# Decays between tokens in the SSD mixer: running sums spread over the partitions by a DMA, in place of triangle products

## The reference, cut to what matters

```python
A_cum = jnp.cumsum(dt * A, axis=2)                        # within a chunk
Acum_t = A_cum.transpose(0, 1, 3, 4, 2)
diff = Acum_t[..., :, None] - Acum_t[..., None, :]
Lmat = jnp.exp(jnp.where(causal, diff, -jnp.inf))         # decay from token s to token l
CB = jnp.einsum('bclgn,bcsgn->bcgls', Cc, Bc)
y_diag = jnp.einsum('bcgrls,bcsgrp->bclgrp', CB[:, :, :, None] * Lmat, xdt)
decay_states = jnp.exp(A_cum[:, :, -1:] - A_cum)
chunk_decay = jnp.exp(A_cum[:, :, -1])
y_off = jnp.einsum('bclgn,bcgrpn->bclgrp', Cc, S_prev) * jnp.exp(A_cum)[..., None]
```

## Time and profile before

| | |
|---|---|
| median of 3 runs | 2328.43 us (2327.97 to 2331.13) |
| the profiled execution | 2326.24 us, its span 2324.4 us |
| mean granted clock of TensorE in it | 0.966 |
| PE busy in the span | 2121.5 us (91%) |
| DVE | 1449.3 us (62%) |
| ACT | 974.8 us (42%) |
| POOL | 502.6 us (22%) |

### The profile page before, as it was taken

One profiled execution on the slowest core, in us unless ns is written; L12 is line 12 of the kernel. 1 busy time (PEld: TensorE's weight loads), 2 busy tenths in 40 slices (PEclk: granted clock), 3 DMA queues, 4 the chain that ended last, 5 costly groups with the idle time before them and its releaser, 6 DMA issues. The chain is left out here.

```text
span 2324.4 us, 43924 instructions
## 1 busy us (share of the span) xinstructions
PE 2121.5 (91%) x15061; PEld 1207.6 (52%) x15062; DVE 1449.3 (62%) x2501; ACT 974.8 (42%) x1470; POOL 502.6 (22%) x378
## 2 busy tenths in 40 slices
PE   7999999999979897999999999659999999999990
PEld 3455554555658873455555555325555555555450
DVE  7566565665668864344445454477566777777763
ACT  5432533333321333222222222147566677667653
POOL 0022121121220000001111011133333443444433
PEclk9999999999989999999999999879999999999995
DMA  8101001011050134112112110089889999999958
GB/s 254 51 28 64 1 28 64 1 28 48 10 227 28 56 127 173 55 37 73 46 64 73 37 46 37 37 305 353 256 277 315 325 342 347 344 336 332 343 167 305
DMA packets 160842, 350.96 MB, mean 151 GB/s; under 512 B 29866, under 2 KB 40490, under 8 KB 160464
## 3 DMA queue, kind: packets, MB, share of 16 engines
q1 hardware_dynamic: 140416, 311.37, 36.8%
q0 software_dynamic: 19152, 33.74, 6.4%
q10 hardware_dynamic: 1152, 4.19, 0.5%
HBM read 299.94 MB, written 58.26 MB: 154 GB/s over the span
## 5 line engine op out<-in xcount | busy, mean ns | idle before, releaser
L2690 PE MATMUL bankE<-wgu,xT 128*64 128x512 f16 x3840 | 429.9, 380 | 20.1 <-issue 11.7
L2690 PEld LDWEIGHTS bankE<-wgu,xT 128*64 128x64 f16 x3840 | 218.3, 110 | 223.1 <-issue 36.7
L2587 DVE SCALAR_TENSOR_TENSOR wgu<-w_rows,wgu 128x2048 f16<-128x2048 f32 x128 | 284.8, 2286 | 37.2 <-ACT wgu L2441 37.1
L111 PE MATMUL bankA<-main_room,hnT 128*128 128x512 f16 (+1 forms) x1536 | 303.2, 355 | 4.1 <-DVE main_room L646 4.1
L2389 POOL DMA_INDIRECT scratch_ybuf<-y,rows x80 | 173.2, 2165 | 376.6 <-DMA scratch_ybuf<-y,rows 276.5
L2441 ACT ACTIVATE wgu<-w_rows 128x2048 f16<-128x2048 f32 x128 | 234.3, 1899 | 34.4 <-issue 27.0
L111 PEld LDWEIGHTS bankA<-main_room,hnT 128*128 128x128 f16 x1536 | 149.9, 98 | 148.5 <-issue 10.3
L2690 PE MATMUL bankE<-wd,hT 128*64 128x512 f16 x1920 | 222.5, 381 | 0.4 <-ACT hT L2472 0.4
L2587 DVE SCALAR_TENSOR_TENSOR wd<-w_rows,wd 128x2048 f16<-128x2048 f32 x64 | 143.8, 2288 | 54.5 <-ACT wd L2441 51.7
L111 PE MATMUL bankA<-hnT,main_room 128*128 128x512 f16 x768 | 169.0, 381 | 8.9 <-issue 6.8
L111 PE MATMUL bankC<-w_out_s,catT 128*128 128x512 f16 x768 | 170.1, 382 | 2.5 <-DVE w_probs L2056 2.5
(11 more groups left out here) (390 smaller groups left out, 2992.1 us busy)
## 6 DMA issues: line engine op xcount, KB each, us to landing
w_rows<-in_w_gate SPq DMA_DIRECT2D x64, 1024.0 KB, 8.3
w_rows<-in_w_up SPq DMA_DIRECT2D x64, 1024.0 KB, 9.6
w_rows<-in_w_down SPq DMA_DIRECT2D x64, 1024.0 KB, 9.1
cat_t<-scratch_cat SPq DMA_DIRECT2D x16, 512.0 KB, 4.8
main_room<-in_x SPq DMA_DIRECT2D x16, 512.0 KB, 5.6
scratch_ybuf<-main_room SPq DMA_DIRECT2D x16, 512.0 KB, 2.6
out<-hf SPq DMA_DIRECT2D x16, 512.0 KB, 11.1
x_room<-in_x SPq DMA_DIRECT2D x3, 2048.0 KB, 10.9
```

Of the source, the lines that this page charges most:

```text
L111: ins = pe.matmul(o, a[x][k], b[y][k], start=start and k == 0 and j == 0, stop=stop and k == n - 1 and j == 2)
L2587: dve.scalar_tensor_tensor(place(p, slot, 1), room(p), W_SCALE, place(p, slot, 0), ALU.mult, ALU.subtract).then_inc(done, 1)
L2690: ins = pe.matmul(o(half), tokens(x, k), rows(z, k, half), start=k == 0 and j == 0, stop=k == n - 1 and j == 2, skip_group_check=True)
```

## The change

The running sums of a chunk are computed a second time as a row for each head: one product with `dtA` as the held operand and the triangle as the moving one gives 8 rows of 128 tokens. DVE copies the 8 rows out of PSUM, SP stores them (4 KB) into memory and loads them back onto all 128 partitions (512 KB, into `E`). ACT copies the running sums per token from PSUM into `cum`. DVE subtracts `cum` from the spread rows, head by head, cut at zero from above (8 operations), and ACT takes one exponential of 1024 columns in place. The triangle products, their two banks' turns in `BY`, and the laid out triangle go. The row of a group's first chunk is computed between the projections `project_vg` and `project_z` of that chunk; those of the other chunks in `retained` of the chunk before. SP's loop over groups is written out. A table of gains, 128 columns, becomes 2 columns that are read repeatedly.

```diff
-        SML = 12
+        SML = 10
-        gam = sb("gam", [P, 2 * RD])
+        gam = sb("gam", [P, 2])
+        cum = sb("cum", [P, SH])
+        row_own = sb("row_own", [SH, P])
...
-        BY = ["act", "act", "act", "act", "act", "dve", "dve", "dve", "dve", "dve", "dve", "dve"]
+        BY = ["act", "act", "act", None, None, "dve", "dve", "dve", "dve", "dve", "dve", "dve"]
...
+            def spread(q):
+                sp.wait_ge(row_taken, q + 1)
+                if q:
+                    sp.wait_ge(row_ld, q * 16)
+                sp.dma_start(row_scr.rearrange("(h l) -> h l", h=SH), row_own[:, :]).then_inc(row_st, 16)
+                sp.wait_ge(row_st, q * 16 + 16)
+                if q:
+                    sp.wait_ge(small, q * SML)
+                sp.dma_start(E[:, :, :].rearrange("p h l -> p (h l)"), row_scr.partition_broadcast(P)).then_inc(row_ld, 16)
...
             def decays(q):
                 act.wait_ge(small, q * SML + 3)
+                act.activation(cum[:, :], bank[SB0 + 2][:, 2 * SN:2 * SN + SH], ACT.Copy)
                 act.activation(dec[:, :, :], bank[SB0 + 2][:, 2 * SN:2 * SN + 3 * SH].rearrange("p (a b) -> p a b", a=3), ACT.Exp)
...
-            def segments(q):
-                for h in range(2):
-                    act.wait_ge(small, q * SML + 4 + h)
-                    act.activation(E2[:, h, :], bank[SB0 + h][:, :], ACT.Exp).then_inc(s_act, 1)
+            def exps(q):
+                act.wait_ge(diffs, q + 1)
+                act.activation(E[:, :, :], E[:, :, :], ACT.Exp).then_inc(e_done, 1)
...
-            def segments(q):
+            def take_row(q, room):
+                if q:
+                    dve.wait_ge(row_st, q * 16)
+                dve.tensor_copy(row_own[:, :], room).then_inc(row_taken, 1)
+
+            def first_row(q):
+                dve.wait_ge(row_done, q // GC + 1)
+                take_row(q, bank[SB0][0:SH, 0:P])
+
+            def differences(q):
+                dve.wait_ge(s_act, q * N_ACT + 3)
+                dve.wait_ge(row_ld, q * 16 + 16)
+                for h in range(SH):
+                    ins = dve.tensor_scalar(E[:, h, :], E[:, h, :], cum[:, h:h + 1], 0.0, ALU.subtract, ALU.min)
+                ins.then_inc(diffs, 1)
...
-                dve.tensor_tensor(segin[:, :, :], bc(le, 1, SH), bc(dtA[:, q % GC, :], 2, P), ALU.mult).then_inc(seg_ready, 1)
...
             def steps_decayed(q):
-                dve.wait_ge(s_act, q * N_ACT + 5)
+                dve.wait_ge(s_act, q * N_ACT + 3)
...
                 dve.wait_ge(s_dve, d0 + 1)
+                dve.wait_ge(e_done, q + 1)
...
+                if c < GC - 1:
+                    take_row(q + 1, bank[SB0][0:SH, RW:RW + P])
                 dve.tensor_copy(Y[:, c, 0:RW], bank[SB0][:, 0:RW]).then_inc(s_dve, 1)
...
-            def segments(q):
-                pe.wait_ge(seg_ready, q + 1)
-                for h in range(2):
-
-                    pe.matmul(room(q, 3 + h)[:, :], gt, sg2[:, h, :], start=True, stop=True).then_inc(small, 1)
+            def row(q, o):
+                pe.wait_ge(dt_ready, q + 1)
+                return pe.matmul(o, dtA[:, q % GC, :], le, start=True, stop=True)
+
+            def first_row(q):
+                row(q, room(q, 0)[0:SH, 0:P]).then_inc(row_done, 1)
...
+                if c < GC - 1:
+                    row(q + 1, o[0:SH, RW:RW + P])
...
+                    if part is project_vg:
+                        first_row(q0)
```

More of the change, by code:

```diff
@@ L375, in _ @@
                 sp.dma_start(late[kt % N_LR], w_in[kt * P:(kt + 1) * P, LATE]).then_inc(l_ld[kt % N_LR], 16)
-            with sp.Fori(0, NG - 1) as g:
+            def spread(q):
[7 more added lines that the diff above has]
+                sp.dma_start(E[:, :, :].rearrange("p h l -> p (h l)"), row_scr.partition_broadcast(P)).then_inc(row_ld, 16)
+            for g in range(NG - 1):
                 sp.wait_ge(big, g * BIG + KT)
-                sp.dma_start(xg[:, :, :], xv[bass.ds(g + 1, 1)].squeeze(0)).then_inc(x_ld, 16)
+                sp.dma_start(xg[:, :, :], xv[g + 1]).then_inc(x_ld, 16)
+                for c in range(GC):
+                    spread(g * GC + c)
                 sp.wait_ge(qk_free, g * GC + GC)
-                sp.dma_start(rope[:, :, :], rv[bass.ds(g + 1, 1)].squeeze(0)).then_inc(r_ld, 16)
+                sp.dma_start(rope[:, :, :], rv[g + 1]).then_inc(r_ld, 16)
                 sp.wait_ge(taken, g * BIG + BIG - 2)
-                sp.dma_start(uv[bass.ds(g, 1)].squeeze(0), dtu[:, :, SH:]).then_inc(u_st, 16)
+                sp.dma_start(uv[g], dtu[:, :, SH:]).then_inc(u_st, 16)
                 sp.wait_ge(out_done, g * GC + GC)
-                sp.dma_start(catv[bass.ds(g, 1)].squeeze(0)[:, :, 0:RW + SW], Y[:, :, :]).then_inc(cat_st, 16)
+                sp.dma_start(catv[g][:, :, 0:RW + SW], Y[:, :, :]).then_inc(cat_st, 16)
             sp.wait_ge(big, (NG - 1) * BIG + KT)
             begun.params(sp)
+            for c in range(GC):
+                spread((NG - 1) * GC + c)
             sp.wait_ge(taken, NG * BIG - 2)
@@ L559, in _ @@
                     take_hn(g, 3)
-                    segments(q0 - 1)
-                    for kt in range(4, KT):
+                    take_hn(g, 4)
+                    exps(q0 - 1)
+                    for kt in range(5, KT):
                         take_hn(g, kt)
@@ L626, in conv @@
                 if g:
-                    dve.wait_ge(small, (g * GC - 1) * SML + (2 if ct < 4 else 6 if ct < 6 else 8))
+                    dve.wait_ge(small, (g * GC - 1) * SML + (2 if ct < 4 else 4 if ct < 6 else 6))
                 if ct < 2:
@@ L722, in weights @@
                 ch.wait()
-                dve.wait_ge(small, s0 + 7)
+                dve.wait_ge(small, s0 + 5)
                 dve.tensor_tensor(PT[:, :, :], bank[SB0][:, :].rearrange("p (a b) -> p a b", a=RH), bc(le, 1, RH), ALU.mult).then_inc(s_dve, 1)
@@ L728, in states @@
                 s0 = q * SML
-                dve.wait_ge(small, s0 + 8)
+                dve.wait_ge(small, s0 + 6)
                 dve.tensor_tensor(yo.rearrange("p (h e) -> p h e", h=SH), bank[SB0 + 1][:, :].rearrange("p (h e) -> p h e", h=SH),
@@ L734, in states @@
                 ch.wait()
-                dve.wait_ge(small, s0 + 9)
+                dve.wait_ge(small, s0 + 7)
                 dve.tensor_tensor(S_m[:, :, :], S_m[:, :, :], bank[SB0 + 2][:, :].rearrange("p (h e) -> p h e", h=SH), ALU.add).then_inc(s_dve, 1)
@@ L814, in _ @@
                     dt_rest(q + 1)
+                    differences(q)
                     rotate(q + 1)
@@ L908, in turn_qk_x @@
                 o = room(q, 0)
+                if c == 0:
+                    pe.wait_ge(row_taken, q + 1)
                 for k in range(4):
@@ L1031, in _ @@
             q = NCH - 1
-            for part in (turn_qk_x, decays, segments, inner, states, retained, results):
+            for part in (turn_qk_x, decays, inner, states, retained, results):
                 part(q)
```

32 lines of the change are left out of this document (15 added, 17 removed).

## The result

The changed kernel took 2337.17 us (median of 7 runs, 2334.85 to 2340.86), the kernel before 2328.43 (7 runs, 2319.14 to 2331.13). The ratio is 1.0045, with a 95% interval of 1.003 to 1.0059: slower, by more than the 0.2% that can be told from no change. The forecast was 2337.7. The profiled execution has a span of 2336.7 us (before 2324.4) and a mean granted clock of 0.958 (before 0.966).

What follows compares the result with a forecast made beforehand. PE was taken as the bound, with DVE nearly as late. Terms -3.8 - 2.9 + 5.1 + 9.1 + 1.8 = +9.3 us gave 2335.5 for the profiled execution, 2337.7 for the median; range 2329 to 2347.

Steps and rivals of the forecast that it cites:

- The price of the subtractions: DVE ahead of the rotation: 0.283 us for one, 1.67 for eight, between 0.77 and 2.2.
- Rival (b): DVE's eight subtractions don't overlap at all: 2.2 us for the eight, kernel at 2346.5 us; chance 0.07.
- The first row: Group openings: PE waits 2.1 us for step sizes in groups 1 and 2; with four row products, 5.1 us lost.
- The turns: Last chunk of a group, among the next group's turns: DVE bounds, 3.04 us lost, three times, 9.1 in all.
- The last chunk: Very last chunk, nothing projected beside it: 1.8 us lost on the path to the next stage, between 1.4 and 2.6.
- The gain inside a group: Twelve chunks beside projections: PE gains 3.8 us in groups' first chunks and 2.9 in the other eight.
- The other two chunks: Eight later chunks beside projections: POOL slows DVE, rotation 1.22 us late, PE gains 0.36 each, 2.9 in all.
- (c): Convolution's first projection at the turns: PE's longer idling lowers its clock, 2 x 1.5 us more, 2340.7; chance 0.14.
- (a): DVE has room inside the groups: subtractions as cheap as the smallest operations, rotation hardly late, 2323.7 us; chance 0.14.
- (d): Spread load of the row late: at 18 us it comes 3.6 us late in 15 chunks, some 2385; chance 0.07.

Runs made afterwards that it cites:

- The sixth: Changed kernel with one subtraction in place of eight in each chunk, so that seven heads' decays are wrong; 2323.23 us, 0.9988 of the kernel before.
- the third experiment: Changed kernel with rotation and masked products ahead of the subtractions in twelve chunks, next group's normalization behind the chunk's work; 2327.9 us, 1.0001 of the kernel before.
- The fifth experiment: Changed kernel with unread matmuls filling PE's waits: 14 and 9 at each turn, 8 ahead of each group's first row; 2331.09 us, 1.0017 of the kernel before.

## Why the prediction was right, point by point

The forecast of 2337.7 lies 0.5 us from the median; the profiled execution, for which the sum gave 2335.5, took 2338.5. That it came so near is luck. The sum was +9.3 us and the stage lost 9.9, but two of the terms were mis-sized, by 5.3 and 6.7 us in opposite directions. Without the loss to the clock, which the sum did not hold at all, some 3 us would have been left, no longer to be told from no change.

- **The price of the subtractions** held: 0.283 us for one and 1.67 for eight were predicted, 0.283 and 1.65 measured. Start to start they are (1.65 - 0.283) / 7 = 0.195 us apart, so that each begins some 0.09 us before the one ahead has ended. Rival (b), no overlap at all and a sum of +18 us, is out. The Trainium skill (VectorE: DVE Perf Modes, The DRAIN you can't avoid) has the next operation wait until the pipe is empty, and adds that one which is not held starts earlier. The trace agrees with the addition, by these 0.09 us, and the prediction had left it out.
- **The first row** held: 2.00 us in groups 1 and 2 alone, where 2.1 was said. (It stands between the third and the fourth projection; the prediction's "second and third" is a slip, its sum counts three.) The row itself sets the next projection back by 0.31 us (249.51 to 249.82) where 0.22 was said.
- **The turns** came to 2.58 us each, 3.04 predicted. DVE stood idle 1.04 where I said 1.18, and ACT's copy did not delay the decayed steps at all: they start 7.32 us after the turn of the chunk's queries and keys, 7.43 before.
- **The last chunk**: 1.85 against 1.8, with the subtractions at 2.00 beside POOL.
- **The gain inside a group, the first mis-sized term**: 12.0 us, 6.7 predicted. In a group's first chunk I said 1.00 and 1.24 came; in the other eight 0.36 and 0.92 came. PE's wait of 1.09 us is the same in all twelve chunks, where I had 1.3 and 1.7: the rotation came 0.57 us late everywhere, not 0.80 and 1.22. (1.80 less 0.57 is the 1.24 to rounding; in the other chunks the row product takes 0.31 of it.) The failed step is the one in "The other two chunks" that took over a DVE as POOL had slowed it in the kernel before, and added ACT's lateness and the subtractions. The decayed steps start 3.17 us after the q,k projection in the second chunk (286.59 to 289.76) as in the first (259.40 to 262.57); I had 3.61. DVE's small operations ahead of them lost 1.6 to 1.8 us beside POOL before (three of them took 0.58, 1.19 and 0.58 us, or two 0.70 and 1.20, for 0.17 each elsewhere) and 1.3 to 1.4 after (1.12 and 0.57), as POOL's operations now fall elsewhere in the chunk (see the last section). They end while ACT is still at its table load, and DVE waits 0.18 us for ACT after them: ACT's lateness alone sets the decayed steps. The other 0.2 of the difference, in a group's first chunk too, is overlap of one operation with the next, from the decayed steps to the rotation. The sixth and the third experiment agree on the size: 0.57 of 1.4 us reaches PE.
- **The clock, the second**: I gave it a rival's place, (c), 0.14 and +3 us, and the sum has nothing for it. It came in full and more: 6.7 us. The condition was right (all three turns fell), and so was the sign; the price was taken from a place where the clock fell for a part of the projection only the earlier trace rows, and the z projection behind a first row was not thought of. Nor was group 0's opening, which the prediction reads as three equal projections: in 70 to 78 us there the kernel before already had 0.55 and 0.59. The fifth experiment is the proof: with PE busy and the waits unchanged, all five projections run at the full clock. The Trainium skill (TensorE: Matmul & The Clock Gate, Part 1) says that idleness throttles the array; the runs agree, and add how often, below.
- **Rivals (a) and (d)** fell: the subtractions are not as cheap as the smallest operations, and the spread load landed in 3.6 us, less than the 6.2 us of a load half its size. DVE's subtractions waited 0.1 us in all.

So the mechanism held (PE spared, DVE late, losses at the groups' ends), the in-group gain was 5.3 us too small, the clock's cost 6.7 too small, the turns 1.4 too large.

## What to carry to other kernels

Work moved from the bound engine to one with idle time costs where that engine's idle time is absent: price it for each kind of place in the program, and then look whether the new work can stand behind what the bound engine waits for. Here two reorderings, one later product and the last chunk's order turned +9 us into -28 against the kernel before, and 11 of these the kernel before could have had by the order alone. A wait of the bound engine costs its length, and here often its clock behind it as well.

## What the runs showed of the hardware that was not expected

- How surely the lower clock follows a wait of PE depends on more than its length. Behind the pair of waits at a turn (2.2 to 3.6 us, then 1.3 to 2.3) the first projection was slow in 15 of 15 places in five runs (6.63 to 8.19 us for 5.34); behind 0.12 and then 2.28 in 1 of 3; behind 0.9 at most and then 0.34 or less it was fast in 12 of 12. Behind the 2.0 us ahead of a first row the z projection was slow in 6 of 10. Behind 4.1 us ahead of group 0's opening the clock was low in 6 of 6 executions, behind 2.8 there in 1 of 4. In two profiled executions of the changed kernel the same four places fell, with lengths equal to within 0.04 us; where edits had shifted the program, other z projections did.
- DVE's smallest operations take 0.17 us, but the one at 286.19 took 1.12 and ended at 287.31, as POOL's normalization ended at 287.29 (order of time on POOL after, below). It is so each time: of the step sizes' small operations 19 are longer than 0.25 us before and 16 after, each began while a POOL operation of the normalization ran and ended 0.02 to 0.03 us after it, and none that began beside one kept its 0.17. In the last chunk the eight subtractions took 2.00 in place of 1.65, and the whole difference lies in the first, 0.63 us, which began beside POOL. No run takes POOL's work away, so that it is the cause is read from the traces alone.

```profile
286.03 1.26 POOL L454 TENSOR_TENSOR Y<-Y,ng_bc 128x512 f32<-128x512 f32 x1
```

- A 4 KB row read by 128 partitions, 512 KB in all, landed in 3.6 us (median of sixteen).
